# Down projections of two MLPs as seven block products in phases, in a two-block float32 transformer kernel

## The reference, cut to what matters

```
u = square(relu(h @ w_up))          # 1024x1024 @ 1024x4096
x = x + rmsnorm(u @ w_down)         # first block:  1024x4096 @ 4096x1024
x = layer_norm(ALPHA*x + u @ w_mlp2)   # second block, the same product
```

## Time and profile before

| what | value |
|---|---|
| median of 3 runs | 2733.04 us |
| profiled execution, its own time | 2732.32 us |
| its span in the trace | 2730.5 us |
| PE matmul busy | 2681.1 us, 98% |
| DVE, ACT, POOL busy | 1394.0, 953.8, 194.2 us |
| instructions on PE | 12432 matmuls |
| down projection, first block | about 1225 to 1588 us |
| down projection, second block | about 2357 to 2715 us |

### The profile page before, as it was taken

One profiled execution on the slowest core, in us unless ns is written; L12 is line 12 of the kernel. 1 busy time (PEld: TensorE's weight loads), 2 busy tenths in 40 slices (PEclk: granted clock), 3 DMA queues, 4 the chain that ended last, 5 costly groups with the idle time before them and its releaser, 6 DMA issues.

```text
span 2730.5 us, 31398 instructions
## 1 busy us (share of the span) xinstructions
PE 2681.1 (98%) x12432; PEld 2157.2 (79%) x12432; DVE 1394.0 (51%) x2148; ACT 953.8 (35%) x1566; POOL 194.2 (7%) x161
## 2 busy tenths in 40 slices
PE   7999999999999999999999999999999999999997
PEld 6766788887888778888888877966788888888886
DVE  4323123334435876654555544155478666466655
ACT  4333222223223565552000242356346665500001
POOL 0000000000021100000000110133020000000002
PEclk9999999999999999999999999999999999999999
DMA  4111211112322345455444321011314445644432
GB/s 163 62 62 62 70 39 39 40 39 100 116 77 105 119 154 170 154 196 209 169 165 150 129 102 52 24 30 26 116 64 152 162 155 170 231 171 173 157 124 108
DMA packets 98162, 314.60 MB, mean 115 GB/s; under 512 B 11072, under 2 KB 11328, under 8 KB 91232
## 3 DMA queue, kind: packets, MB, share of 16 engines
q1 hardware_dynamic: 98016, 312.59, 33.2%
HBM read 217.06 MB, written 92.34 MB: 113 GB/s over the span
## 4 chain that ended last, share of the span: by engine, by line
PE 79%; issue 14%; DVE 3%; DMA 2%; POOL 1%; ACT 1%; SPq 0%; POOLq 0%; ACTq 0%; DVEq 0%
PE bank L567 23%; PE bank L569 23%; PE bank L568 23%; PE bank L1013 2%; PE bank L701 1%; PE bank L964 1%; POOL accX L2288 1%; POOL accX L2279 1%; PE bank L990 1%; PE bank L678 1%; PE bank L991 1%; PE bank L965 1%; DVE wlo L1594 1%; PE bank L745 1%; PE bank L628 1%
## 5 line engine op out<-in xcount | busy, mean ns | idle before, releaser
L567 PE MATMUL bank<-whi,ub 128*128 128x512 f32 x1024 | 404.8, 395 | 1.6 <-DMA ub<-ud_d 0.8
L569 PE MATMUL bank<-whi,ub 128*128 128x512 f32 x1024 | 404.0, 395 | 0.0
L568 PE MATMUL bank<-wlo,ub 128*128 128x512 f32 x1024 | 404.0, 395 | 0.0
L1594 DVE TENSOR_TENSOR wlo<-raw,whi 128x1024 fp32r<-128x1024 f32 x166 | 202.1, 1236 | 384.3 <-ACT whi L1053 383.8
L1053 ACT ACTIVATE whi<-raw 128x1024 fp32r<-128x1024 f32 x166 | 171.2, 1053 | 635.9 <-PE bank L569 623.8
L1843 DVE TENSOR_TENSOR accX<-bank,accX 128x512 f32<-128x512 f32 x288 | 194.0, 689 | 144.5 <-PE bank L569 144.1
L567 PE MATMUL bank<-hhi,whi 128*128 128x512 f32 x608 | 251.6, 414 | 2.0 <-DVE hlo L1619 2.0
L569 PE MATMUL bank<-hhi,wlo 128*128 128x512 f32 x608 | 238.6, 392 | 0.0
L568 PE MATMUL bank<-hlo,whi 128*128 128x512 f32 x608 | 238.1, 392 | 0.0
L567 PEld LDWEIGHTS bank<-whi,ub 128*128 128x128 f32 x1024 | 192.9, 188 | 47.8 <-issue 1.7
L569 PEld LDWEIGHTS bank<-whi,ub 128*128 128x128 f32 x1024 | 192.9, 188 | 45.2
(11 more groups left out here) (372 smaller groups left out, 5523.4 us busy)
## 6 DMA issues: line engine op xcount, KB each, us to landing
raw<-wp_d SPq DMA_DIRECT2D x166, 512.0 KB, 3.6
ub<-ud_d SPq DMA_DIRECT2D x64, 1024.0 KB, 8.5
ud_d<-h SPq DMA_DIRECT2D x128, 256.0 KB, 2.9
ud_d<-l SPq DMA_DIRECT2D x128, 256.0 KB, 3.3
rawp<-wp_d SPq DMA_DIRECT2D x26, 1024.0 KB, 6.2
gs<-sg_d SPq DMA_DIRECT2D x16, 512.0 KB, 3.9
xd_d<-accX SPq DMA_DIRECT2D x16, 512.0 KB, 2.6
sg_d<-sig SPq DMA_DIRECT2D x13, 512.0 KB, 2.6
```

What stands on the lines that cost most here:

```text
L567: e.matmul(P, sh, mh, start=first, stop=False, skip_group_check=more)
L568: e.matmul(P, sh, ml, start=False, stop=False, skip_group_check=more)
L569: return e.matmul(P, sl, mh, start=False, stop=last, skip_group_check=more)
L1594: e.tensor_tensor(out=wlo[n % SLOTS][:, :], in0=raw[n % RAWS][:, :], in1=whi[n % SLOTS][:, :].bitcast(F32), op=ALU.subtract).then_inc(*up( ...
```

## The change: what it does

Both down projections become seven block products. u (1024 tokens x 4096) and W (4096 x 1024) are cut in 2x2 blocks: token halves, halves of the hidden dimension, output halves. For this the 16 pairs of hidden chunks (3 plain ones, 13 of the up projection) hold one chunk of each hidden half. A phase is one block product over all 16 pairs; it has 8 steps of two pairs. A step is, for each of 4 token tiles, two chunks x 3 matmuls, so 24 matmuls; 56 steps are 1344 matmuls. Steps are numbered 0 to 55.

- The seven u operands are S1, S2, S3, A22, A11, A12, S4. The up projection no longer splits u: ACT makes relu and square, DVE makes the four sums (sums_of_u) in place of the low parts, and SP stores 7 tiles of 256 KB a pair in place of 8. For the plain chunks the blocks are stored, read back, summed and stored again in pairs 2 to 4 (std_again, sums_of_std, std_sums_out).
- In the down projection each step fetches 512 KB of u (ra, 3 buffers) and one or two raw pieces of W (two in phases 0 and 2). DVE makes the difference of W blocks in phases 0 to 3 (w_sum). ACT then makes the high parts of u and W (u_high, w_high), DVE the low parts (u_low, w_low). The split parts have three buffers.
- A phase adds up in 4 banks. Phases 1, 2 and 3 use banks 4 to 7 one after the other without clearing between them, phases 4 and 5 too; phase 6 goes on in banks 0 to 3 where phase 0 left off. At a phase's end ACT copies the banks out (phases 0, 1, 3, 4, 5) or DVE adds them to the accumulator (2 and 6). The result of phase 4 is added to three blocks in steps 40 to 43 (p1_added).
- The last two steps are interleaved by token tile. Tiles 0 to 3 are normalized during phase 6 (early), tiles 4 to 7 after each finished tile of its end (late). The next block's first raw pieces share memory with ra and are fetched after step 55's u has been split.

```diff
-def down_pieces(G):
-    return [2 * G, 2 * G + 1] if G < 14 else [28, 29, 30, 31]
+S1, S2, S3, A22, A11, A12, S4, A21 = range(8)
+PHASES = 7
+STEPS_DOWN = 8 * PHASES
+W_BLOCKS = ((1, 0), (3,), (3, 1), (2,), (0,), (2,), (3,))
+PHASE_BANK = (0, 4, 4, 4, 4, 4, 0)
+PHASE_ADDS = (False, False, True, True, False, True, True)
...
+# PE
+            def step_of(s, t):
+                if t == 0:
+                    e.wait_ge(*ok("bl", tag, s))
+                if step == 0:
+                    P, free = ring.open("dn" + tag, phase, t, bank=PHASE_BANK[phase] + t)
+                    e.wait_ge(*free)
+                for j in range(2):
+                    i = mm3(P[:, :], ah[:, j, c], al[:, j, c], bh[:, j, :], bl[:, j, :], ...)
...
+            for t in range(4):
+                step_of(STEPS_DOWN - 2, t)
+                step_of(STEPS_DOWN - 1, t).then_inc(*ring.full("dn" + tag, PHASES - 1, t))
+                late()
...
+# ACT
+            def u_high(s):
+                e.wait_ge(*ok(f"ra{s % 3}", tag, s))
+                if s > 2:
+                    e.wait_ge(*ok("dns", tag, s - 3))
...
+            for i in range(STEPS_DOWN):
+                if i + 2 < STEPS_DOWN:
+                    u_high(i + 2)
+                    w_high(i + 2)
+                if i % 8 == 7:
+                    phase_end(i // 8)
+                if STEPS_DOWN - 8 <= i < STEPS_DOWN - 1:
+                    early()
+                if i == STEPS_DOWN - 2:
+                    feed.cap = min(feed.cur + 2, NPIECES)
+                    feed.ahead(feed.cap)
+            for t in range(4):
+                late()
...
+# DVE
+            for i in range(STEPS_DOWN):
+                if i + 2 < STEPS_DOWN:
+                    if i + 2 < 32:
+                        w_sum(i + 2)
+                    u_low(i + 2)
+                    w_low(i + 2)
+                if i == 23:
+                    for t in range(4):
+                        e.wait_ge(*ok("full", "dn" + tag, 2, t))
+                        e.wait_ge(*ok("free", "dn" + tag, 0, t))
+                        add_to(t, 1, bank_of("dn" + tag, 2, t)[:, :], *free("dn" + tag, 2, t))
+                if 40 <= i < 44:
+                    p1_added(i - 40)
+                if residual and 44 <= i < 48:
+                    residual(i - 44)
+                if residual and 49 <= i < 53:
+                    residual(i - 45)
+                if STEPS_DOWN - 8 <= i < STEPS_DOWN - 1:
+                    early()
...
+# SP
+            def fetch_u(s):
+                if s > 2:
+                    e.wait_ge(*ok("al", tag, s - 3))
...
+            def fetch_w(s):
+                for r, block in zip(w_fetches(s), W_BLOCKS[phase]):
+                    if r < 8:
+                        e.wait_ge(*ok("full", ("sc" if r > 3 else "sb") + tag, last, 0))
+                    elif r < 16:
+                        e.wait_ge(*ok("bl", tag, s - 4))
+                    elif r < 48:
+                        e.wait_ge(*ok("bl", tag, s - 1 if phase == 3 and step < 4 else s - 4))
+                    else:
+                        e.wait_ge(*ok("bl", tag, s - 2))
...
+                if 12 <= t < 12 + NT:
+                    reload(t - 12)
+                if t == STEPS_DOWN - 2:
+                    e.wait_ge(*ok("al", tag, STEPS_DOWN - 1))
+                    feed.cap = NPIECES
+                    feed.ahead(feed.cur)
```

More of the change, by code:

```diff
@@ L882, in mlp @@
[L882 to L888, removed]
+            def step_of(s, t):
+                phase, step = divmod(s, 8)
+                ah, al, bh, bl = parts_uw(s)
+                c = slice(128 * t, 128 * t + 128)
+                if t == 0:
[3 more added lines that the diff above has]
+                    e.wait_ge(*free)
+                P = bank[PHASE_BANK[phase] + t]
+                for j in range(2):
+                    i = mm3(P[:, :], ah[:, j, c], al[:, j, c], bh[:, j, :], bl[:, j, :], not PHASE_ADDS[phase] and step == 0 and j == 0,
+                            step == 7 and j == 1, PHASE_ADDS[phase])
+                return i
@@ L1377, in strassen @@
                 else:
[L1378 to L1385, removed]
+                    u_high(0)
+                    u_high(1)
+                squared_11(p)
                 if more:
@@ L1420, in mlp @@
                 strassen(p)
[L1421 to L1427, removed]
-        def y_square(t):
-            e.wait_ge(*ok("free", "dna", 14, t, 1))
+            squared("21", last, r21, f21)
+            w_high(1)
+            squared("12", last, r12[last % 2], r12[last % 2])
+            for i in range(STEPS_DOWN):
[9 more added lines that the diff above has]
+                    feed.ahead(feed.cap)
+            for t in range(4):
+                late()
+            feed.cap = NPIECES
+        def y_square(t):
+            if t < 4:
+                e.wait_ge(*ok("p1a", "a", t))
+            else:
+                e.wait_ge(*ok("free", "dna", 5, t - 4))
+                e.wait_ge(*ok("free", "dna", 6, t - 4))
             if t:
@@ new lines, in w_sum @@
+            def w_sum(s):
+                phase, step = divmod(s, 8)
+                rs = w_fetches(s)
+                for r in rs:
+                    e.wait_ge(*ok(f"rb{r % 8}", tag, r))
+                if phase == 0:
+                    e.wait_ge(*ok("full", "sb" + tag, last, 1 + step // 4))
+                dst = raw_w(rs[0]) if phase == 2 else Tw[step]
+                in1 = raw_w(rs[1]) if len(rs) == 2 else Tw[step]
+                e.tensor_tensor(out=dst[:, :], in0=raw_w(rs[0])[:, :], in1=in1[:, :], op=ALU.subtract).then_inc(*up("tw", tag, s))
```

468 lines of the change are left out of this document (292 added, 176 removed), and 6 rows, old and new, of the table CHAINS.

## The result

The changed kernel takes **2654.6 us** (median of 4 runs, 2650.44 to 2654.99) against 2733.39 us before (2732.76 to 2733.83): a ratio of 0.971, 95% interval 0.969 to 0.973, or 78.8 us less. 2662 us was predicted, 2645 to 2683 as the range. The profiled execution took 2654.99 us, with a span of 2652.9 us: 77.6 us less than the span before.

A forecast was written before the change was run, and what follows sets the result against it. PE, busy 98% of the span at full clock, was taken as the bound. Terms -89.3 - 0.8 + 5.0 + 5.0 + 5.4 + 3.7 = -71.0 us took 2732.3 to 2661.3; the median lies 0.7 above: 2662 us, range 2645 to 2683.

The forecast's parts named there:

- The matmuls removed: Both down projections: 1536 matmuls become 1344 in each, 16 blocks of 12 fewer at 2.79 us, 89.3 us less for both.
- the idle time: Down projections: of 1.6 us that PE idled for the old groups' fetches, half was taken as gone, 0.8 us less.
- Steady steps: Down projection steps of 5.58 us: DVE, ACT and fetches stay hidden, 7 us spare, cost 0.
- start: From pair 12 into the first down steps: parts ready just in time, cost 0, bounds 0 and 3 us per MLP.
- The rival in which thin margins break: Starts, seams and ends cost more and fetches lag: 21 us on top of 2662, so 2683 us; chance 0.24.
- The seam: Phases 2 to 3, steps 23 to 24: PE waits for DVE's adds behind chained W fetches, 2.5 us per MLP, 5.0 both.
- The first block's end: After step 55: late raw pieces and in-order splits delay tile 4 through POOL; PE waits, cost 5.0 us, bounds 0 and 8.
- The second block's end: From step 50: a closed ACT and DVE round of 8.0 us against 5.58; PE waits 5.4 us, bounds 0 and 8.
- The tail: After the last product: the last four tiles end closer together, last bias at 16.0 us; cost 3.7 us, bounds 1 and 6.
- the same spacing of 0.2325 us: Sign to show the forecast right: PE with 12048 matmuls, still 0.2325 us from start to start as before.

The follow-up runs named there:

- the three repairs: Changed kernel with phase 3's W fetched four steps ahead, next stage's first two splits later at first block's end, second block's root, scaling and bias later: 2639.32 us.

## Why the prediction was right, point by point

*The matmuls removed (-89.3) and the idle time (-0.8).* The count was exact. At the pace of the kernel before, the product holds. Of the 1.6 us of idle time nearly all went, not half: the wait for ub is gone and that for wlo fell from 3.8 to 3.1 us, 1.5 in all.

*Steady steps and start (0).* Right in this trace: PE waits for no part in phases 0 to 2, though DMA moves 303 GB/s there. But the margin at the start was gone. Step 3's low part of W ended at 1239.40 us and PE took it at 1239.46, where the working had 1.4 us to spare, and in four variants PE waited there, 0.2 to 1.1 us. The rival in which thin margins break came that near.

*The seam (+5.0).* 2.4 and 2.3 us, so 4.7.

*The first block's end (+5.0).* 5.8 us, by the queue that was described. POOL's tile was ready 53.1 us after the start of step 48, just as worked out; the wait is longer because PE, with its faster steps, stood there after 47.4 us and not 48.2. SP's, ACT's and POOL's timelines:
```profile
1527.33 1.73 SPq L2585 DMA_DIRECT2D raw<-wp_d  x3
```
```profile
1532.09 1.06 ACT L1119 ACTIVATE whi<-raw 128x1024 fp32r<-128x1024 f32 x1 [5.22 <-DMA raw<-wp_d]
```
```profile
1539.53 2.35 POOL L2488 TENSOR_TENSOR accX<-accX,acc 128x1024 f32<-128x1024 f32 x1 [16.42 <-DVE acc L2236]
```
ACT stands 5.2 us in front of the piece that SP issued late, two splits go ahead of the add, and POOL receives its tile at the end of that.

*The second block's end (+5.4).* The mechanism is right and the size too small: 7.8 us. The round took 8.5 us, not 8.0. DVE's and POOL's timelines show the difference:
```profile
2585.65 1.23 DVE L2124 TENSOR_TENSOR vw0al<-ra,vw0ah 128x1024 fp32r<-128x1024 f32 x1 [1.22 <-ACT vw0ah L1434]
...
2592.27 1.99 DVE L2124 TENSOR_TENSOR vw1al<-ra,vw1ah 128x1024 fp32r<-128x1024 f32 x1 [1.22 <-ACT vw1ah L1434]
...
2617.24 2.53 DVE L2124 TENSOR_TENSOR vw1al<-ra,vw1ah 128x1024 fp32r<-128x1024 f32 x1 [2.25 <-ACT vw1ah L1434]
```
```profile
2590.77 2.42 POOL L2576 TENSOR_TENSOR accX<-accX,fg 128x1024 f32<-128x1024 f32 x1 [587.04 <-ACT accX L1687]
...
2616.34 2.35 POOL L2576 TENSOR_TENSOR accX<-accX,fg 128x1024 f32<-128x1024 f32 x1 [6.11 <-ACT accX L1687]
```
The first low part has no POOL operation beside it and takes 1.23 us. The second overlaps POOL's by 0.9 us and takes 0.8 longer, the third by 1.4 us and takes 1.3 longer: DVE hardly moves while POOL works. The Trainium skill, page "SBUF — State Buffer", section "Terms", says of the port pair that DVE and GpSimd share that it is held for a whole instruction and that the loser "fully blocks"; the trace agrees to a tenth of a microsecond or two.

*The tail (+3.7).* 19.2 us after the last matmul against 15.3: +3.9. The last bias ended 16.2 us after the last product, 16.0 by the working.

*What had no term.* The pace: 2 x 1344 matmuls x 0.0058 us = -15.6 us. The sentence that failed is the one which makes a step "5.58 us", and with it the sign "the same spacing of 0.2325 us"; it carried a spacing from one pair of buffers to another, and the two kernels with moved regions show that it belongs to the placement. And the half clock after PE's new pauses, read from step lengths: 1.7 and 1.6 us at the seams, 1.5 at the first end, 2.9 at the second, +7.7 us. Together with the terms above: -71.0 - 0.7 - 0.3 + 0.8 + 2.4 + 0.2 - 15.6 + 7.7 = -76.5 us, against -77.6 in the span. The first down product already starts 2.1 us earlier (1223.1 against 1225.2), which is about as much as executions of these kernels differ there; the rest was not taken apart. The forecast was near, then, partly by luck: two unseen effects of opposite sign were added to a good list of stalls, and without the faster pace it would have been some 9 us too low.

## What to carry to other kernels

Write the in-order queues out by hand for every seam, with the fetch that each round waits for: four waits were named and sized so before the run. Where the size was off by most, at the second block's end, an instruction had been taken at its undisturbed length beside POOL. Price a pause of PE above its length: here 2.4 us cost up to 4.3. And before a matmul spacing is carried over to another plan, look where both operands lie; when products of one shape show two paces, move the buffers before anything else is rebuilt.

## What was not expected of the hardware

- A 128x512 matmul follows the one before in 0.2267 us when its weights and its moving tile lie in regions at the same fraction of a KB, and in 0.2325 us when one region is 640 bytes off; the profile's mean shows it as 389 and 395 ns. After a mixed product up to nine matmuls of an aligned one were still uneven. Moving the regions took 28.6 us from the kernel before, 15.0 from the changed one and 13.9 from the one with the three repairs.
- After a pause of PE of 2.1 to 2.7 us the granted clock fell to 0.50 in 11 of 16 cases; it fell between 0.3 us before PE's return and 1.5 us after it, and stayed there for 3.4 us; matmuls were then 0.43 us apart. In the pause of 5.8 us it fell 2.0 us after PE's last matmul, while PE stood. Matmuls without a use, put into that pause, kept it at 1.00.
- An fp32 operation of DVE on two SBUF tensors grew from 1.22 to 2.0 and 2.5 us beside one of POOL.
- DMA moved 375 and 406 GB/s in the 2 us windows from 1358 us above, and 405 over the 15 us of the kernel before in the earlier trace rows.
